# Feed-forward first products: one 512-column matmul for both parts of the activations

## The chip, the cores and the metric

The kernel runs on one core of a Trainium2 chip. The time is the device time of one execution, in microseconds (us); lower is better. The core has a matrix engine (TensorE, PE in the rows), whose weight loads have a row of their own (PEld), a vector engine (VectorE, DVE), a scalar engine (ScalarE, ACT), a third elementwise engine (GpSimd, POOL) and a queue that issues transfers (SyncE, SP). Each engine works off its own instructions in program order and waits on semaphores for the others.

## The reference

Activations are 256 tokens of 1024 channels. There are three layers with mixers of different kinds (a gated delta rule with pooling, a spatial gating unit, RWKV-7), and behind each mixer stands a feed-forward with a squared ReLU. The change concerns the three feed-forwards only:

```
D_MODEL = 1024
D_FF = 4 * D_MODEL
    ...
    u = rms_norm(h, norm_mlp[l])
    h = h + jnp.square(jax.nn.relu(u @ w_up[l])) @ w_down[l]
    ...
def _squared_relu_mlp(h, w1, w2):
    return jnp.square(jax.nn.relu(h @ w1)) @ w2
```

All inputs are float32.

## The kernel before

**Split products.** Matmul operands are rounded to a shorter format (float32r). To keep accuracy each operand is held as two such parts, a high part (the rounded value) and a low part (what the rounding left). A product is three matmuls: low weights by high activations, high weights by low activations, high by high. `split_matmul` (L2082 to L2086) issues them, all three into the same 256 columns of a PSUM bank; each loads its 128x128 weight tile anew.

**Units.** All weights come in units of 128 x 2048 numbers (1 MB) through a ring of four buffers. For each unit SyncE transfers it into `raw`, ScalarE rounds it to `w_high` (`high`, L660), VectorE forms `w_low` (`low`, L1237), TensorE uses it and counts `w_used`. `high(u)` waits until TensorE has used unit u-4, since the two share a buffer.

**A feed-forward.** The 4096 hidden channels go in 8 chunks of 512. A chunk has two up units (s = 0 and 1, two hidden tiles of 128 channels each, 8 input tiles deep, so 16 tile products of three matmuls, 48 in all) and two down units (`accumulate`, also 16 tile products). From unit u0 the ring holds: up chunk 0 (u0, u0+1), up chunk 1 (u0+2, u0+3), down chunk 0 (u0+4, u0+5), up chunk 2, down chunk 1, and so on. TensorE works in that order: `body(i)` does up chunk i+1, then down chunk i. The up results lie in banks 0 (s = 0) and 1 (s = 1), the down sums in banks 2 to 5; bank 6 takes the sum of squares for the token scale.

**Between the two products.** For each half s of a chunk ScalarE's `relu` (L862, L874 for chunk 0) takes the bank to `FB.r`, and with that the bank is free. VectorE's `hidden` squares it to `FB.h` (L1556), ScalarE's `square` makes the high part (L869), VectorE the low part (L1561). An up unit of chunk i+1 waits for `relu_done` of chunk i, half s.

**VectorE's order.** It is written out by hand. `mlp` does `low` of u0+2 and u0+3, halves the squares, does `low` of u0+4 and u0+5, and then for each chunk `body(i)`: `hidden(i)`, then `low` of the next four units: up chunk i+2 (two), down chunk i+1 (two). So `hidden(i)` stands behind the `low` of both down units of chunk i. In the second feed-forward `scale_lora` (L1618 to L1626) and the low part of a LoRA weight (L1581) stand between some chunks. ScalarE has the same order: `square` twice, `high` twice (up chunk i+2), `relu` twice (chunk i+1), `high` twice (down chunk i+1).

## Time and profile before

| | us |
|---|---|
| median of 3 runs | 1057.31 |
| lowest and highest | 1056.78, 1058.25 |
| span of the profiled execution (first to last instruction) | 1055.0 |
| TensorE matmul busy in it | 1038.3 |
| VectorE busy | 715.8 |
| ScalarE busy | 536.1 |

The profile is of one execution, whose span is 2.3 us under the median of the timed runs. Ends of matmuls are modelled and overlap, so TensorE's pace is read from the starts of its matmuls. Between first and last a timeline row gives start, length, engine, line and tiles; "x2" is two instructions of the same kind in a row, and the bracket behind a row is the idle time ahead of it and what ended it.

### The profile page before, as it was taken

The numbers are of one execution on the slowest core, as the hardware profiler recorded it, in microseconds if no ns is written. First come the engines' busy times: TensorE is split into PE (matmuls) and PEld (weight loads), VectorE is DVE, ScalarE is ACT, GpSimd is POOL, SyncE is SP. The second block draws the span as 40 slices with busy tenths as digits, with TensorE's granted clock in tenths as the row PEclk, the third lists the DMA queues.
The fourth block names the chain that finished last, engine by engine and source line by source line (L and its number), as shares of the span: only waits on it lengthen the run. The fifth ranks groups of instructions, "written<-read, shape, count | busy, mean of one in ns | idle before, by whom it ended". The sixth has DMA issues, their size and how long they took to land.

```text
span 1055.0 us, 21161 instructions
## 1 busy us (share of the span) xinstructions
PE 1038.3 (98%) x8984; PEld 1008.7 (96%) x8984; DVE 715.8 (68%) x1007; ACT 536.1 (51%) x639; POOL 32.6 (3%) x39
## 2 busy tenths in 40 slices
PE   7999999999999999999999999999999999999997
PEld 7999999999997899999999999999898999999997
DVE  6989665455567787666565567899978666555454
ACT  7847553434446464355445346897543255443431
POOL 0004000000000000000000000042000000000000
PEclk9999999999999999999999999999999999999999
DMA  9722475546744646565555553424100257555511
GB/s 293 222 81 82 160 262 177 194 166 203 275 157 141 219 160 204 159 186 211 186 172 184 182 191 120 140 73 152 58 2 2 64 179 253 183 189 171 196 40 40
DMA packets 119057, 167.01 MB, mean 158 GB/s; under 512 B 5840, under 2 KB 99664, under 8 KB 118608
## 3 DMA queue, kind: packets, MB, share of 16 engines
q1 hardware_dynamic: 117808, 165.92, 47.9%
q8 instruction: 48, 0.79, 0.3%
q10 hardware_dynamic: 1184, 0.17, 0.1%
q14 instruction: 17, 0.14, 0.0%
HBM read 165.03 MB, written 1.05 MB: 157 GB/s over the span
## 4 chain that ended last, share of the span: by engine, by line
PE 84%; DVE 10%; ACT 2%; issue 2%; SPq 1%; DMA 1%; DVEq 0%; ACTq 0%
PE banks L2084 25%; PE banks L2086 25%; PE banks L2085 24%; DVE sb_w_low L1237 2%; DVE sb_arena L1917 1%; DVE sb_state L1914 1%; DMA sb_raw<-in_w_in 1%; PE banks L2668 1%; PE banks L2535 1%; SPq L539 1%; PE banks L2779 0%; DVE sb_arena L1405 0%; DVE sb_state L1402 0%; PE banks L2838 0%; PE banks L2822 0%
## 5 line engine op out<-in xcount | busy, mean ns | idle before, releaser
L1237 DVE TENSOR_TENSOR sb_w_low<-sb_raw,sb_w_high 128x2048 fp32r<-128x2048 f32 x148 | 338.0, 2289 | 242.1 <-ACT sb_w_high L660 242.0
L660 ACT ACTIVATE sb_w_high<-sb_raw 128x2048 fp32r<-128x2048 f32 x148 | 281.8, 1911 | 262.9 <-PE banks L2086 261.7
L2084 PE MATMUL banks<-sb_act_high,sb_w_low 128*128 128x256 f32 x1352 | 386.3, 286 | 1.1 <-DVE sb_arena L1790 0.7
L2086 PE MATMUL banks<-sb_act_high,sb_w_high 128*128 128x256 f32 x1352 | 381.9, 282 | 0.0
L2085 PE MATMUL banks<-sb_act_low,sb_w_high 128*128 128x256 f32 x1352 | 380.0, 281 | 0.0
L2084 PEld LDWEIGHTS banks<-sb_act_high,sb_w_low 128*128 128x128 f32 x1352 | 254.6, 188 | 3.3 <-DVE sb_arena L1790 0.9
L2085 PEld LDWEIGHTS banks<-sb_act_low,sb_w_high 128*128 128x128 f32 x1352 | 255.9, 189 | 0.5 <-issue 0.2
L2084 PE MATMUL banks<-sb_hidden_high,sb_w_low 128*128 128x256 f32 x896 | 253.6, 283 | 0.0
L2086 PEld LDWEIGHTS banks<-sb_act_high,sb_w_high 128*128 128x128 f32 x1352 | 253.4, 187 | 0.0
L2086 PE MATMUL banks<-sb_hidden_high,sb_w_high 128*128 128x256 f32 x896 | 253.4, 283 | 0.0
L2085 PE MATMUL banks<-sb_hidden_low,sb_w_high 128*128 128x256 f32 x896 | 251.9, 281 | 0.0
L2085 PEld LDWEIGHTS banks<-sb_hidden_low,sb_w_high 128*128 128x128 f32 x896 | 169.5, 189 | 0.1
L2084 PEld LDWEIGHTS banks<-sb_hidden_high,sb_w_low 128*128 128x128 f32 x896 | 168.9, 189 | 0.1
L2086 PEld LDWEIGHTS banks<-sb_hidden_high,sb_w_high 128*128 128x128 f32 x896 | 167.8, 187 | 0.0
L1561 DVE TENSOR_TENSOR sb_hidden_low<-sb_arena,sb_hidden_high 128x512 fp32r<-128x512 f32 x48 | 31.2, 686 | 11.3 <-ACT sb_hidden_high L869 11.3
L869 ACT ACTIVATE sb_hidden_high<-sb_arena 128x512 fp32r<-128x512 f32 x48 | 27.6, 618 | 20.4 <-PE banks L2086 20.4
L1556 DVE TENSOR_TENSOR sb_arena<-sb_arena 128x512 f32<-128x512 f32 x48 | 30.7, 681 | 0.0
L2084 PE MATMUL banks<-sb_w_high,sb_act_low 128*128 128x512 f32 x64 | 26.3, 411 | 0.0
L2086 PE MATMUL banks<-sb_w_high,sb_act_high 128*128 128x512 f32 x64 | 25.4, 396 | 0.0
L2085 PE MATMUL banks<-sb_w_low,sb_act_high 128*128 128x512 f32 x64 | 25.3, 396 | 0.0
L633 POOL TENSOR_SCALAR sb_arena<-sb_arena 128x256 f32<-128x256 f32 x8 | 10.7, 1360 | 421.5 <-ACT sb_act_high L986 421.5
L862 ACT ACTIVATE sb_arena<-banks 128x512 f32<-128x512 f32 x42 | 22.3, 583 | 0.0
(443 smaller groups left out, 1048.6 us busy)
## 6 DMA issues: line engine op xcount, KB each, us to landing
sb_raw<-in_ffn_w SPq DMA_DIRECT2D x64, 1024.0 KB, 5.2
sb_raw<-in_w_up SPq DMA_DIRECT2D x16, 1024.0 KB, 5.4
sb_raw<-in_w_down SPq DMA_DIRECT2D x16, 1024.0 KB, 5.0
sb_raw<-in_sgu_w_in SPq DMA_DIRECT2D x16, 1024.0 KB, 5.3
sb_raw<-in_rwkv_w_rkv SPq DMA_DIRECT2D x12, 1024.0 KB, 5.2
sb_raw<-in_w_in SPq DMA_DIRECT2D x8, 1024.0 KB, 9.6
sb_raw<-in_sgu_w_out SPq DMA_DIRECT2D x8, 1024.0 KB, 4.9
sb_raw<-in_w_out SPq DMA_DIRECT2D x4, 1024.0 KB, 5.1
```

The costliest lines, as they stand in the source:

```text
L539: sp.dma_start(half_of(raw[j], t), w_in_v[:, :, c * 256 + t * P:c * 256 + t * P + P])\
L633: pool.tensor_scalar(RW.XS[:, k, :], RW.H[:, k, 1:T + 1], RW.omm[:, p:p + 1], None, ALU.mult)\
L660: nc.scalar.activation(whi[s][:], raw[s][:], ACT.Copy).then_inc(hi_done, 1)
L862: nc.scalar.activation(FB.r[:, 2 * s:2 * s + 2, :], two(bank[s][:]), ACT.Relu).then_inc(relu_done, 1)
L869: nc.scalar.activation(hid_hi[:, 2 * s:2 * s + 2, :], FB.r[:, 2 * s:2 * s + 2, :], ACT.Square)\
L1237: nc.vector.tensor_tensor(wlo[s][:], raw[s][:], f32(whi[s][:]), ALU.subtract).then_inc(lo_done, 1)
L1556: nc.vector.tensor_tensor(FB.h[:, hs, :], FB.r[:, hs, :], FB.r[:, hs, :], ALU.mult).then_inc(r_sq, 1)
L1561: nc.vector.tensor_tensor(hid_lo[:, hs, :], FB.h[:, hs, :], f32(hid_hi[:, hs, :]), ALU.subtract)\
L1914: base.add(nc.vector.tensor_tensor(tmp, RW.LB[:, j + 1:, j:j + 1].broadcast_to(shape), RW.WB[:, j:j + 1, 0:j + 1].broadcast_to(shape), ALU ...
L2084: nc.tensor.matmul(dst, l_lo, r_hi, start=start, stop=False, **kw)
L2085: nc.tensor.matmul(dst, l_hi, r_lo, start=False, stop=False, **kw)
L2086: return nc.tensor.matmul(dst, l_hi, r_hi, start=False, stop=stop, **kw)
```

## The change

The high and the low part of the activations become one tensor (`act_parts`). In an up unit each high weight tile is loaded once and meets both parts in one matmul of 512 columns, whose result fills a whole bank: high by high in the left 256 columns, high by low in the right. The low weights by high activations, 256 columns, are added to the right half. A half s of a chunk has two hidden tiles and thus takes two banks: 0 and 1 for s = 0, 6 and 7 for s = 1. The sum of squares moves to bank 5, which is also a down bank; so the first down unit waits at its seventh output tile until VectorE has taken the scale (`scale_taken`), and VectorE takes it in its first body, not in its last but one.

Behind the product ScalarE copies the right halves of both banks to `FB.r` (512 columns, as `relu` had), VectorE adds the left halves to it from PSUM (new, 48 instructions) and counts `up_taken`, then does ReLU and square in one instruction, ScalarE copies that to the high part, VectorE forms the low part. TensorE's up unit of chunk i+1 now waits for `up_taken` of chunk i, half s.

```diff
@@ scalar
-            def relu(i, s):
+            def copy_half(i, s):
                 act.wait_ge(w_used, i * 4 + (u0 - 2 + s + 1))
                 act.wait_ge(h_lo, i * 2 + (h0 - 2 + s + 1))
-                nc.scalar.activation(FB.r[:, 2 * s:2 * s + 2, :], two(bank[s][:]), ACT.Relu).then_inc(relu_done, 1)
-
-            def square(i, s):
-
-                act.wait_ge(relu_done, i * 2 + (16 * j + s + 1))
+                nc.scalar.activation(FB.r[:, 2 * s:2 * s + 2, :], up_halves[s][:, :, 1, :], ACT.Copy).then_inc(up_copied, 1)
+
+            def hidden_high(i, s):
+
+                act.wait_ge(r_sq, i * 2 + (16 * j + s + 1))
                 if not (type(i) is int and i == 0):
                     act.wait_ge(w_used, i * 4 + (u0 + s + 1))
-                nc.scalar.activation(hid_hi[:, 2 * s:2 * s + 2, :], FB.r[:, 2 * s:2 * s + 2, :], ACT.Square)\
+                nc.scalar.activation(hid_hi[:, 2 * s:2 * s + 2, :], FB.h[:, 2 * s:2 * s + 2, :], ACT.Copy)\
                     .then_inc(h_hi, 1)
@@ vector
             def hidden(i, then=lambda s: None):
                 for s in range(2):
                     hs = slice(2 * s, 2 * s + 2)
-                    dve.wait_ge(relu_done, i * 2 + (16 * j + s + 1))
-                    nc.vector.tensor_tensor(FB.h[:, hs, :], FB.r[:, hs, :], FB.r[:, hs, :], ALU.mult).then_inc(r_sq, 1)
+                    dve.wait_ge(up_copied, i * 2 + (16 * j + s + 1))
+                    nc.vector.tensor_tensor(FB.r[:, hs, :], FB.r[:, hs, :], up_halves[s][:, :, 0, :], ALU.add)\
+                        .then_inc(up_taken, 1)
+                for s in range(2):
+                    hs = slice(2 * s, 2 * s + 2)
+                    dve.wait_ge(up_taken, i * 2 + (16 * j + s + 1))
+                    nc.vector.scalar_tensor_tensor(FB.h[:, hs, :], FB.r[:, hs, :], 0.0, FB.r[:, hs, :], ALU.max,
+                                                   ALU.mult).then_inc(r_sq, 1)
...
-            def body(i, last):
+            def body(i, last, first=False):
                 hidden(i)
                 low(u0 + 6, i)
+                if first:
+                    token_scale()
                 low(u0 + 7, i)
@@ tensor
+                if n == 6 and scales is not None:
+                    pe.wait_ge(scale_taken, scales)
...
                 if i is not None:
-                    pe.wait_ge(relu_done, i * 2 + (16 * j + s + 1))
+                    pe.wait_ge(up_taken, i * 2 + (16 * j + s + 1))
                 for t in range(2):
                     for k in range(KT):
                         if first and t == 0 and s == 0:
                             pe.wait_ge(a_lo, a0 + k + 1)
-                        cs = slice(t * P, t * P + P)
-                        ins = split_matmul(bank[s][:, t * T:t * T + T], h[:, k, cs], l[:, k, cs], act_hi[:, k, :],
-                                           act_lo[:, k, :], start=k == 0, stop=k == KT - 1)
+                        cs, dst = slice(t * P, t * P + P), bank[UP_BANKS[s] + t]
+                        nc.tensor.matmul(two(dst[:]), h[:, k, cs], act_parts[:, :, k, :], start=k == 0,
+                                         stop=False, skip_group_check=True)
+                        ins = nc.tensor.matmul(dst[:, T:2 * T], l[:, k, cs], act_hi[:, k, :], start=False,
+                                               stop=k == KT - 1, skip_group_check=True)
```

TensorE, head of its loop over the chunks of the first feed-forward, from the last matmuls of down chunk 0 into up chunk 2; `relu` is the semaphore of `relu_done`. Before:

```order
L2085 MATMUL banks<-sb_hidden_low,sb_w_high 128x256
L2086 MATMUL banks<-sb_hidden_high,sb_w_high 128x256
L2474 UNCONDITIONAL_BRANCH
L2474 ISA
L2451 ISA [waits unit_low]
L2084 MATMUL banks<-sb_act_high,sb_w_low 128x256 [waits relu]
L2085 MATMUL banks<-sb_act_low,sb_w_high 128x256
L2086 MATMUL banks<-sb_act_high,sb_w_high 128x256
```

The same place in the changed kernel:

```order
L2102 MATMUL banks<-sb_hidden_low,sb_w_high 128x256
L2103 MATMUL banks<-sb_hidden_high,sb_w_high 128x256
L2495 UNCONDITIONAL_BRANCH
L2495 ISA
L2470 ISA [waits unit_low]
L2476 MATMUL banks<-sb_act_parts,sb_w_high 128x512 [waits up_taken]
L2478 MATMUL banks<-sb_act_parts,sb_w_low 128x256
```

Three matmuls of a tile product have become two, and the wait on ScalarE's `relu` has become one on VectorE's `up_taken`.

VectorE, first feed-forward, from `low` of the two units of down chunk 0 to the first chunk's `hidden` and the `low` behind it (`unit_high` is ScalarE's `high`, `hidden_hi` its high part of the hidden values). Before:

```order
L1237 TENSOR_TENSOR sb_w_low<-sb_raw,sb_w_high 128x2048 [waits unit_high] x2
L1584 UNCONDITIONAL_BRANCH
L1584 ISA
L1556 TENSOR_TENSOR sb_arena<-sb_arena 128x512 [waits relu]
L1555 REGISTER_ALU
L1556 TENSOR_TENSOR sb_arena<-sb_arena 128x512 [waits relu]
L1561 TENSOR_TENSOR sb_hidden_low<-sb_arena,sb_hidden_high 128x512 [waits relu_squared,hidden_hi] x2
L1236 ISA
L1237 TENSOR_TENSOR sb_w_low<-sb_raw,sb_w_high 128x2048 [waits unit_high]
```

The same place in the changed kernel:

```order
L1241 TENSOR_TENSOR sb_w_low<-sb_raw,sb_w_high 128x2048 [waits unit_high] x2
L1560 TENSOR_TENSOR sb_arena<-sb_arena,banks 128x512 [waits up_copied] x2
L1565 SCALAR_TENSOR_TENSOR sb_arena<-sb_arena 128x512 [waits up_taken] x2
L1571 TENSOR_TENSOR sb_hidden_low<-sb_arena,sb_hidden_high 128x512 [waits relu_squared,hidden_hi] x2
L1241 TENSOR_TENSOR sb_w_low<-sb_raw,sb_w_high 128x2048 [waits unit_high]
L1578 TENSOR_SCALAR sb_arena<-banks 128x256 [waits square_sums]
L1581 RECIPROCAL sb_arena<-sb_arena 128x256 [waits token_scale_taken]
L1241 TENSOR_TENSOR sb_w_low<-sb_raw,sb_w_high 128x2048 [waits unit_high] x3
```

The two adds that free the banks have come in at the place of the squares, behind the `low` of both down units; the token scale stands in the first body.

## Rows read from the trace of the kernel before

**Rows 1.** The page: busy time of the engines, share of the span, instructions.
```profile
PE 1038.3 (98%) x8984; PEld 1008.7 (96%) x8984; DVE 715.8 (68%) x1007; ACT 536.1 (51%) x639; POOL 32.6 (3%) x39
```

**Rows 2.** The page: the chain that ended last, by engine.
```profile
PE 84%; DVE 10%; ACT 2%; issue 2%; SPq 1%; DMA 1%; DVEq 0%; ACTq 0%
```

**Rows 3.** Groups by line: out<-in, count | busy us, mean ns | idle before, releaser.
```profile
L1237 DVE TENSOR_TENSOR sb_w_low<-sb_raw,sb_w_high 128x2048 fp32r<-128x2048 f32 x148 | 338.0, 2289 | 242.1 <-ACT sb_w_high L660 242.0
...
L1556 DVE TENSOR_TENSOR sb_arena<-sb_arena 128x512 f32<-128x512 f32 x48 | 30.7, 681 | 0.0
...
L1598 DVE TENSOR_TENSOR sb_arena<-banks,sb_arena 128x512 f32<-128x512 f32 x11 | 7.6, 689 | 10.8 <-PE banks L2086 10.8
...
L1689 DVE SCALAR_TENSOR_TENSOR sb_arena<-banks,sb_gating_scales,sb_arena 128x512 f32<-128x512 f32 x8 | 5.6, 744 | 0.0
```

**Rows 4.** Timeline, TensorE: first and 48th matmul of one up unit.
```profile
208.25 0.28 PE L2084 MATMUL banks<-sb_act_high,sb_w_low 128*128 128x256 f32 x1
...
213.89 0.28 PE L2086 MATMUL banks<-sb_act_high,sb_w_high 128*128 128x256 f32 x1
```

**Rows 5.** Timeline, TensorE: first and 93rd of the spatial gate's 512-column matmuls.
```profile
337.96 0.39 PE L2085 MATMUL banks<-sb_w_low,sb_act_high 128*128 128x512 f32 x1
...
359.50 0.40 PE L2084 MATMUL banks<-sb_w_high,sb_act_low 128*128 128x512 f32 x1
```

**Rows 6.** Timeline, TensorE: 256 columns behind 8-column weight loads, first and 22nd.
```profile
23.02 0.28 PE L2086 MATMUL banks<-sb_act_high,sb_ab_high 128*8 128x256 f32 x1
...
25.41 0.28 PE L2086 MATMUL banks<-sb_act_high,sb_ab_high 128*8 128x256 f32 x1
```

**Rows 7.** Timeline, ScalarE and VectorE around one chunk's `hidden`, loop of feed-forward 1.
```profile
198.75 1.06 ACT L862 ACTIVATE sb_arena<-banks 128x512 f32<-128x512 f32 x2
...
208.45 1.92 ACT L660 ACTIVATE sb_w_high<-sb_raw 128x2048 fp32r<-128x2048 f32 x1 [3.85 <-PE banks L2086]
...
210.40 2.29 DVE L1237 TENSOR_TENSOR sb_w_low<-sb_raw,sb_w_high 128x2048 fp32r<-128x2048 f32 x1 [3.47 <-ACT sb_w_high L660]
212.61 1.29 DVE L1556 TENSOR_TENSOR sb_arena<-sb_arena 128x512 f32<-128x512 f32 x2
```

**Rows 8.** Timeline, entry of feed-forward 1: TensorE's unit u0+2 begins; ScalarE; VectorE.
```profile
138.70 0.28 PE L2084 MATMUL banks<-sb_act_high,sb_w_low 128*128 128x256 f32 x1
...
139.39 3.71 ACT L660 ACTIVATE sb_w_high<-sb_raw 128x2048 fp32r<-128x2048 f32 x2
...
141.33 4.50 DVE L1237 TENSOR_TENSOR sb_w_low<-sb_raw,sb_w_high 128x2048 fp32r<-128x2048 f32 x2 [2.36 <-ACT sb_w_high L660]
145.75 1.29 DVE L1556 TENSOR_TENSOR sb_arena<-sb_arena 128x512 f32<-128x512 f32 x2
```

**Rows 9.** Timeline, VectorE in feed-forward 2: work between `low` and `hidden`.
```profile
521.53 2.29 DVE L1237 TENSOR_TENSOR sb_w_low<-sb_raw,sb_w_high 128x2048 fp32r<-128x2048 f32 x1 [3.47 <-ACT sb_w_high L660]
...
526.45 1.29 DVE L1556 TENSOR_TENSOR sb_arena<-sb_arena 128x512 f32<-128x512 f32 x2
...
546.78 2.42 DVE L1626 TENSOR_TENSOR sb_arena<-sb_arena,sb_vectors 128x512 f32<-128x512 f32 x3
...
569.82 2.28 DVE L1581 TENSOR_TENSOR sb_lora_low<-sb_arena,sb_lora_high 128x2048 fp32r<-128x2048 f32 x1
```

**Rows 10.** Timeline: a VectorE result and the TensorE matmul that waited for it.
```profile
860.53 0.48 DVE L1502 SCALAR_TENSOR_TENSOR sb_act_low<-sb_x,sb_vectors,sb_act_high 128x256 fp32r<-128x256 f32 x1
...
861.06 0.39 PE L2084 MATMUL banks<-sb_act_high,sb_w_low 128*128 128x256 f32 x1 [0.37 <-DVE sb_act_low L1502]
```

**Rows 11.** Windows (from:to length, PE busy (count), granted clock, DMA share, GB/s): the end.
```profile
1048.40:1051.30 2.90, 0.03 (x1) 1.00 0.14 47
1051.30:1055.00 3.70, 0.00 (x0) 0.50 0.75 247
```

**Rows 12.** Timeline, TensorE: first matmuls of the program; the last ones.
```profile
5.36 5.23 PE L2193 MATMUL banks<-sb_x,sb_ones 128*128 128x256 f32 x12 [5.36 <-DMA sb_x<-in_x_t]
...
1046.75 1.67 PE L2967 MATMUL banks<-sb_arena,sb_ones 128*128 128x256 f32 x7
```

More of the change, by code:

```diff
@@ L145, in place @@
         return nc.alloc_sbuf_tensor_at("sb_" + name, shape, dtype, offset=at + 4 * offset)
-    act_hi = place("act_high", 0, [P, KT, T], F32R)
-    act_lo = place("act_low", UNIT, [P, KT, T], F32R)
+    act_parts = place("act_parts", 0, [P, 2, KT, T], F32R)
+    act_hi, act_lo = act_parts[:, 0], act_parts[:, 1]
     hid_hi = place("hidden_high", 2 * UNIT, [P, 4, T], F32R)
@@ L355, in build_on @@
     FFN_ACC = [0, 6, 9]
+    UP_BANKS = [0, 6]
+    up_halves = [banks[:, 512 * b:512 * b + 1024].rearrange("p (t h n) -> p t h n", t=2, h=2) for b in UP_BANKS]
     ACC_SGU = 3
@@ L873, in mlp @@
                 act.wait_ge(w_used, u0 + s + 1)
-                nc.scalar.activation(FB.r[:, 2 * s:2 * s + 2, :], two(bank[s][:]), ACT.Relu).then_inc(relu_done, 1)
+                nc.scalar.activation(FB.r[:, 2 * s:2 * s + 2, :], up_halves[s][:, :, 1, :], ACT.Copy).then_inc(up_copied, 1)
             high(u0 + 4)
@@ L879, in body @@
                 for s in range(2):
-                    square(i, s)
+                    hidden_high(i, s)
                 high(u0 + 6, i)
@@ L889, in body_end @@
             def body_end(s):
-                square(FCH - 1, s)
+                hidden_high(FCH - 1, s)
                 if u0 + 4 * FCH < n_units:
@@ L1563, in hidden, with token_scale @@
                     then(s)
-            def body(i, last):
+            def token_scale():
+                dve.wait_ge(ss_done, SS[("ffn1", "ffn2", "ffn3")[j]] + 1)
+                nc.vector.tensor_scalar(FB.r2[j], bank[5][:, 0:T], 1.0 / D, EPS, ALU.mult, ALU.add)\
+                    .then_inc(scale_taken, 1)
+                dve.wait_ge(scale_taken, j + 1)
+                chain.add(nc.vector.reciprocal(FB.r2[j], FB.r2[j]))
+            def body(i, last, first=False):
                 hidden(i)
                 low(u0 + 6, i)
+                if first:
+                    token_scale()
                 low(u0 + 7, i)
@@ L1574, in mlp @@
                 for i in range(FCH - 2):
-                    body(i, False)
+                    body(i, False, first=i == 0)
                     if i in (1, 2):
@@ L1583, in mlp @@
             else:
-                with dve.Fori(0, FCH - 2) as i:
+                body(0, False, first=True)
+                with dve.Fori(1, FCH - 2) as i:
                     body(i, False)
-            dve.wait_ge(ss_done, SS[("ffn1", "ffn2", "ffn3")[j]] + 1)
-            chain.add(nc.vector.tensor_scalar(FB.r2[j], bank[6][:, 0:T], 1.0 / D, EPS, ALU.mult, ALU.add))
-            chain.settle()
-            chain.add(nc.vector.reciprocal(FB.r2[j], FB.r2[j]))
             body(FCH - 2, True)
@@ L2424, in _, with accumulate @@
             mixed_out(c, range(4, KT))
-        def accumulate(u, s, i=None, first=False, last=False):
+        def accumulate(u, s, i=None, first=False, last=False, scales=None):
             q = u % RING
@@ L2465, in body @@
                     pe.wait_ge(sq_folded, j + 1)
-                    nc.tensor.matmul(bank[6][:, 0:T], ones, FB.ss[j], start=True, stop=True).then_inc(ss_done, 1)
+                    nc.tensor.matmul(bank[5][:, 0:T], ones, FB.ss[j], start=True, stop=True).then_inc(ss_done, 1)
                 for s in range(2):
                     pe.wait_ge(h_lo, i * 2 + (h0 + s + 1))
-                    accumulate(u0 + 4 + s, s, i, first=first and s == 0)
+                    accumulate(u0 + 4 + s, s, i, first=first and s == 0, scales=j + 1 if first and s == 0 else None)
             up(u0, 0, first=True)
```

5 lines of the change are left out of this document (3 added, 2 removed).

## The prediction

> **What bounds the kernel now.** I read the page first. TensorE is busy 98% of the span, VectorE 68%, ScalarE 51% [rows 1], and the chain of work that ended last runs through TensorE for 84% [rows 2]. So the kernel goes at TensorE's pace, and a change is worth what it does to the starts of matmuls. Next, the timeline of one up unit: 48 matmuls of 256 columns, the first at 208.25, the last at 213.89, so 5.64/47 = 0.1200 us from start to start [rows 4]. No pause lies between the last down unit and this one. ScalarE and VectorE, on the other hand, wait: VectorE's `low` waited 242 us in all for ScalarE's `high` [rows 3], and the `high` at 208.45 had waited 3.85 us for TensorE to give its buffer back [rows 7]. This is slack, but it has a consequence for the order of things: the `high` and `low` of a down unit are tied to the moment at which TensorE finishes the down unit four earlier.
>
> **The merged matmuls.** A tile product was three matmuls, 3 x 0.1200 = 0.360 us. It becomes one of 512 columns and one of 256. The spatial gate has 512-column matmuls in the same format: 92 steps from 337.96 to 359.50, 0.2341 us each [rows 5]. So a tile product takes 0.2341 + 0.1200 = 0.3541 us, 5.9 ns less. There are 3 feed-forwards x 16 up units x 16 = 768, which gives 4.5 us. What goes is the part of a weight load that isn't hidden: behind loads of 8 columns the same 256-column matmul takes 2.39/21 = 0.1138 us [rows 6], 6.2 ns less than behind 128. The bounds: nothing, if the two separate runs of 256 columns in `act_parts` cost the 512-column matmul what it saves (a contiguous operand is all that rows 5 show); and 2 x 6.2 ns x 768 = 9.5 us, if the other load also vanishes behind the longer matmul. I take 4.5, since rows 5 measure it directly. The first 8 tile products of each feed-forward wait for activations anyway, so about 0.1 us of it is lost: 4.4.
>
> The Trainium skill (TensorE: Matmul & The Clock Gate, Back-to-back issue gap) gives for isolated matmuls a time of columns over 2.4 GHz plus 2.5 ns. By that a merged pair saves 2.5 ns, or 1.9 us in all, and my final sum would be 2.6 us higher; rows 4 and 5 (120.0 and 234.1 ns against its 109.2 and 215.8) lie above it, and I go by the rows.
>
> **The work that is added.** VectorE gets 48 adds out of PSUM, about 0.69 us each (same shape, L1598), and its 48 squares become instructions with three operands, 0.74 against 0.68 us [rows 3]: 33 + 3 = 36 us on an engine with 339 us idle. By volume this is hidden, since TensorE needs 23.0 us for a chunk (192 x 0.12) and VectorE some 12 (four `low` of 2.29 and four short ones). ScalarE's copies have the shapes of the ReLU and the square before and take their places.
>
> **The wait that is exchanged.** Here the time is decided. Up unit (i+1, s) may start only when the results of chunk i, half s, have left their banks. Before, ScalarE's ReLU did that, right behind the up unit and long before. Now VectorE's add does it, and that stands in `hidden(i)`, behind `low` of the two down units of chunk i. The second of these needs `high` of the same unit, and this needs TensorE to have finished the second down unit of chunk i-1. But this is the unit directly ahead of up unit (i+1, 0). So TensorE finishes a down unit, and the next thing it wants has yet to go through ScalarE (`high`), VectorE (`low`) and VectorE (add), one behind the other. What stands queued behind the waiting matmul is the whole rest of TensorE's program.
>
> The length is read off where these instructions already stand. In the loop, TensorE wants to start the up unit at 208.25 [rows 4]. ScalarE's `high` ran from 208.45, `low` from 210.40, and the squares, in whose place the adds come, from 212.61 [rows 7]. With 0.69 for an add the first bank pair is free at 213.30. From the end of a VectorE result to the matmul that waited for it lie 0.05 us (860.53 + 0.48 = 861.01, matmul at 861.06) [rows 10]. So TensorE restarts at 213.35: a **stall of 5.1 us**. The second half is free 0.6 us after the first, under cover of the 5.7 us of the first up unit. It happens for i = 1 to 6 in each of three feed-forwards: 18 x 5.1 = 91.8 us.
>
> At the entry (i = 0) TensorE wants unit u0+2 at 138.70. VectorE has `low` of u0+4 and u0+5 ahead, which end at 145.83, since ScalarE made their high parts in 139.39 to 143.10; the add would run from 145.75 to 146.44, the restart at 146.49 [rows 8]. That is 7.8 us; the entries of the other two feed-forwards show the same offsets. 3 x 7.8 = 23.4 us.
>
> In feed-forward 2 more work stands between `low` and `hidden`: from 521.53 to 526.45 are 4.92 us, where the loop has 2.21 (210.40 to 212.61), so 2.7 more; the second group of three (2.42, net 2.3) and two LoRA low parts (2.28, net 2.2 each) follow in the next three chunks [rows 7, 9]. Together 9.4 us. The stalls sum to 91.8 + 23.4 + 9.4 = **124.6 us**.
>
> That the engine can't slip the adds in earlier is what the rows show: the squares at 212.61 had had their input since ScalarE's two ReLUs ended at 199.8 and still ran behind the `low` [rows 7]. The Trainium skill (TensorE: Matmul & The Clock Gate, Architectural detail) has the same as a rule against the change: VectorE and ScalarE take their queues strictly in order. By that the stalls are certain; with a free order the sum would be that of the first rival.
>
> **The clock.** After the last matmul, whose modelled end is 1048.4, the granted clock stood at 1.00 until 1051.3 and then fell to 0.50 [rows 11], 1.2 GHz in place of 2.4, 2.9 us after work had stopped. The stalls are 5.1 us and more, so it will mostly fall in them. What comes back how fast, only the start shows: the first twelve matmul instructions started 0.44 us apart ((5.23 - 0.4)/11), from 5.36 to about 10.2, the last ones of the same form 0.22 apart ((1.67 - 0.38)/6, with 0.38 for the length of one) [rows 12]: 4.9 us at half pace, 2.4 us lost. Per stall the loss is between 0 (clock stays, or falls just as work resumes and returns at once) and 2.4. I take 1.7, nearer the upper end, since the stall is nearly twice the 2.9 us but a restart need not meet the full 4.9. 21 x 1.7 = **35.7 us**; bounds 0 and 50.4.
>
> The Trainium skill (same page, Part 1: The HAM clock gate) says that throttled is the default and activity releases it; with that rule alone the loss would be above zero at each of the 21 restarts.
>
> **Edits at nothing.** The first down unit waits at its seventh tile for `scale_taken`. That is 36 x 0.12 = 4.3 us after its start, while the sum of squares is ready at its start, and VectorE by then waits for the next `high`; covered, and if not, under 2 us each, three times. The longer way to the low part of the hidden values (copy, add, square, copy, low part, some 3.4 us) lies beside the up units of chunk i+1, 11.3 us, which start only after the first add. No transfer moves on SyncE's queue; each is due a chunk ahead.
>
> **Sum**, against the profiled execution: 1055.0 - 4.4 + 124.6 + 35.7 = 1210.9 us of span; with the 2.3 us by which the median lies above it, **1213 us**.
>
> **Rivals.**
> *No stall (faster).* If the adds were reached in time, only the merged matmuls would show: 1057.3 - 4.4 = 1052.9, or between 1047.8 and 1057.3 with the bounds. It decides at one point: VectorE's `low` of a chunk's second down unit would have to end 5.1 us before it does, ahead of the end of the down unit before it. For it: before the change TensorE never waited here, and VectorE is idle a third of the time. Against: rows 7, where idle time is all ahead of `low` and not ahead of the squares. 6%.
> *Stalls, but the clock stays.* 1057.3 - 4.4 + 124.6 = 1177.5. For it: the one fall that the trace has came at a real end, and when in a pause it comes may vary; the start's slow pace might have to do with something else. Against: 2.9 us is well under 5.1, and the row at 0.50 is plain. 12%. A clock that falls in half of the stalls gives about 1195 and belongs to the forecast's range.
> *Stalls, and the full price of the clock at each.* 1213.3 + 14.7 = 1228; if besides each stall is 0.3 us longer (ScalarE or VectorE slower to start than in rows 7), 1234. 12%.
>
> **How the numbers follow.** The forecast, stalls with a clock that mostly falls, has 68% and by itself lies between 1192 and 1228. Another 2% is left for something not seen. For 8 in 10 the range must take in one side case whole: it goes down to 1175 (clock stays) and up to 1236. The measurement can tell about 0.2% (2 us) from no change; only the first rival is not slower, and it is faster by over 0.2% in most of its bounds. Faster 0.05, same 0.02, slower 0.93.
>
> **What would show it.** In the profile of the changed kernel: TensorE waits for VectorE's add (L1560) 21 times, some 125 us in all, none over 9 us; a chunk takes 28 to 30 us where it took 23; within an up unit a tile product takes 0.354 us; granted clock at 0.50 for a stretch behind most stalls. It would be wrong if TensorE's idle time before the merged matmuls is small, if the clock column stays at 1.00, or if up units are slower than 0.36 us per tile product at full clock.

## The result

The changed kernel takes 1228.9 us (median of 4 runs, 1227.1 to 1230.8) against 1057.2 us (4 runs, 1056.8 to 1058.3): a ratio of 1.1621, 95% interval 1.1607 to 1.1635. It is 16% slower. The forecast was 1213 us, the range 1175 to 1236.

The profiled execution has a span of 1227.2 us. Its page: busy time, the granted clock in 40 slices, the chain that ended last by engine, and the costliest group (count | busy us, mean ns | idle before, releaser).

```profile
PE 1088.2 (89%) x8216; PEld 1009.6 (82%) x8216; DVE 747.3 (61%) x1055; ACT 540.0 (44%) x639; POOL 32.6 (3%) x39
...
PEclk9999888888899999988888889999999988888889
...
PE 76%; DVE 13%; ACT 5%; issue 4%; SPq 1%; DMA 1%; DVEq 0%; ACTq 0%
...
L2476 PE MATMUL banks<-sb_act_parts,sb_w_high 128*128 128x512 f32 x768 | 323.0, 453 | 122.1 <-DVE sb_arena L1560 121.7
```

Beside [rows 1, 2]: TensorE's share fell from 98 to 89%, though it has 768 matmuls fewer and more busy time (a slow clock makes each of them longer). In the chain, VectorE and ScalarE together went from 12 to 18%. The clock's row has 8s in three stretches, which are the three feed-forwards. Nearly all idle time of the new matmul has one releaser, the add, and the view of TensorE's waits (total us, times, longest) counts it:

```profile
PE banks L2476 <- DVE sb_arena L1560: 121.7, 21, 7.7
```

The timeline around one of the 21 waits, in the loop of feed-forward 1 (start, length, engine, line, ..., idle time before): TensorE's last matmul of a down unit and its next one; ScalarE; VectorE.

```profile
202.25 0.28 PE L2103 MATMUL banks<-sb_hidden_high,sb_w_high 128*128 128x256 f32 x1
207.45 0.80 PE L2476 MATMUL banks<-sb_act_parts,sb_w_high 128*128 128x512 f32 x1 [4.92 <-DVE sb_arena L1560]
...
202.57 1.91 ACT L664 ACTIVATE sb_w_high<-sb_raw 128x2048 fp32r<-128x2048 f32 x1 [3.84 <-PE banks L2103]
...
204.51 2.29 DVE L1241 TENSOR_TENSOR sb_w_low<-sb_raw,sb_w_high 128x2048 fp32r<-128x2048 f32 x1 [3.46 <-ACT sb_w_high L664]
206.72 1.28 DVE L1560 TENSOR_TENSOR sb_arena<-sb_arena,banks 128x512 f32<-128x512 f32 x2
```

These lines answer to [rows 7]. The chain is to be read from top to bottom: TensorE ends a down unit, this lets ScalarE's `high` start (202.57), then `low` (204.51), then the adds (206.72), and after the first of them TensorE goes on at 207.45. From its last start, 202.25, that is 5.20 us, of which 0.12 would have passed anyway. In the same way the 21 places sum to 127.5 - 21 x 0.12 = 125.0 us of stopped TensorE.

The windows of the same stop (from:to length, PE busy (count), granted clock, DMA share, GB/s):

```profile
202.30:206.30 4.00, 0.23 (x2) 1.00 0.71 256
206.30:207.40 1.10, 0.00 (x0) 0.54 0.00 0
207.40:213.20 5.80, 5.75 (x18) 0.50 0.54 181
213.20:221.40 8.20, 8.20 (x49) 1.00 0.00 0
```

The last matmul's modelled end is 202.53; 3.9 us later the clock fell from 2.4 to 1.2 GHz, and it stayed there for the first 5.8 us of the up unit. Over the 21 stops the fall came 2.4 to 4.6 us behind the last start. Added up from windows of 0.2 us, TensorE worked 114.9 us at the half clock behind the 21 restarts: 3.8 to 6.2 us behind each, 5.5 in the mean.

What the half clock does to a tile product is seen in the same up unit: first two starts at half clock, six tile products apart, then an up unit's first matmul and the one behind its last, 16 tile products apart, at full clock.

```profile
208.26 0.63 PE L2476 MATMUL banks<-sb_act_parts,sb_w_high 128*128 128x512 f32 x1
...
212.10 0.63 PE L2476 MATMUL banks<-sb_act_parts,sb_w_high 128*128 128x512 f32 x1
...
215.76 0.39 PE L2476 MATMUL banks<-sb_act_parts,sb_w_high 128*128 128x512 f32 x1
...
221.36 0.28 PE L2101 MATMUL banks<-sb_hidden_high,sb_w_low 128*128 128x256 f32 x1
```

3.84/6 = 0.640 us against 5.60/16 = 0.350 us. So of 114.9 us at the half clock a share of 1 - 0.350/0.640 = 0.453 is lost, 52.1 us.

### The profile page after: what moved, and what is told of

Same layout as the page of the kernel before. It is cut to its first block, busy times and chain, and to the rows that moved or that the text cites. A ratio compares the mean times of both kernels' runs of the same rounds, so it can differ in the third digit from the quotient of the medians.

```text
span 1227.2 us, 19655 instructions
## 1 busy us (share of the span) xinstructions
PE 1088.2 (89%) x8216; PEld 1009.6 (82%) x8216; DVE 747.3 (61%) x1055; ACT 540.0 (44%) x639; POOL 32.6 (3%) x39
## 4 chain that ended last, share of the span: by engine, by line
PE 76%; DVE 13%; ACT 5%; issue 4%; SPq 1%; DMA 1%; DVEq 0%; ACTq 0%
PE banks L2476 18%; PE banks L2101 14%; PE banks L2103 13%; PE banks L2102 13%; PE banks L2478 9%; DVE sb_w_low L1241 4%; ACT sb_w_high L664 4%; DVE sb_arena L1560 1%; DVE sb_arena L1934 1%; DVE sb_state L1931 1%; DMA sb_raw<-in_w_in 1%; PE banks L2689 1%; PE banks L2556 1%; SPq L543 1%; DVE sb_arena L1643 0%
## 5 line engine op out<-in xcount | busy, mean ns | idle before, releaser
L2476 PE MATMUL banks<-sb_act_parts,sb_w_high 128*128 128x512 f32 x768 | 323.0, 453 | 122.1 <-DVE sb_arena L1560 121.7
L2476 PEld LDWEIGHTS banks<-sb_act_parts,sb_w_high 128*128 128x128 f32 x768 | 169.8, 221 | 170.1 <-DVE sb_arena L1560 102.2
L2478 PE MATMUL banks<-sb_act_parts,sb_w_low 128*128 128x256 f32 x768 | 237.1, 309 | 0.0
L2101 PE MATMUL banks<-sb_act_parts,sb_w_low 128*128 128x256 f32 x584 | 169.4, 290 | 0.8 <-DVE sb_arena L1807 0.7
L2478 PEld LDWEIGHTS banks<-sb_act_parts,sb_w_low 128*128 128x128 f32 x768 | 170.0, 221 | 0.0
L2103 PE MATMUL banks<-sb_act_parts,sb_w_high 128*128 128x256 f32 x584 | 164.9, 282 | 0.0
L2102 PE MATMUL banks<-sb_act_parts,sb_w_high 128*128 128x256 f32 x584 | 164.0, 281 | 0.0
L2101 PEld LDWEIGHTS banks<-sb_act_parts,sb_w_low 128*128 128x128 f32 x584 | 109.8, 188 | 2.8 <-DVE sb_arena L1807 0.9
L2102 PEld LDWEIGHTS banks<-sb_act_parts,sb_w_high 128*128 128x128 f32 x584 | 110.8, 190 | 0.5 <-issue 0.2
L2103 PEld LDWEIGHTS banks<-sb_act_parts,sb_w_high 128*128 128x128 f32 x584 | 109.4, 187 | 0.0
L1565 DVE SCALAR_TENSOR_TENSOR sb_arena<-sb_arena 128x512 f32<-128x512 f32 x48 | 30.9, 684 | 0.0
L1560 DVE TENSOR_TENSOR sb_arena<-sb_arena,banks 128x512 f32<-128x512 f32 x48 | 30.7, 680 | 0.0
```

The source lines that it names most:

```text
L1560: nc.vector.tensor_tensor(FB.r[:, hs, :], FB.r[:, hs, :], up_halves[s][:, :, 0, :], ALU.add)\
L1565: nc.vector.scalar_tensor_tensor(FB.h[:, hs, :], FB.r[:, hs, :], 0.0, FB.r[:, hs, :], ALU.max, ALU.mult).then_inc(r_sq, 1)
L2101: nc.tensor.matmul(dst, l_lo, r_hi, start=start, stop=False, **kw)
L2102: nc.tensor.matmul(dst, l_hi, r_lo, start=False, stop=False, **kw)
L2103: return nc.tensor.matmul(dst, l_hi, r_hi, start=False, stop=stop, **kw)
L2476: nc.tensor.matmul(two(dst[:]), h[:, k, cs], act_parts[:, :, k, :], start=k == 0, stop=False, skip_group_check=True)
```

## The experiments

All times are medians, beside runs of the kernel before on the same chip (1057.0 to 1057.9 us). "With early adds" is the first kernel below.

### The adds moved ahead

In the changed kernel, VectorE's adds leave `hidden` and stand ahead of the `low` of u0+8. That is the first down unit of chunk i+1 (the expectation has the number right and calls it the second of chunk i), so both `low` that stood ahead of the adds now stand behind them. At a feed-forward's entry, not in the cut below, one add goes ahead of the halving of the squares and one behind it, both ahead of the `low` of u0+4.

```diff
             def hidden(i, then=lambda s: None):
-                for s in range(2):
-                    ... add of the two halves, .then_inc(up_taken, 1)
             def body(i, last, first=False):
                 ...
                 low(u0 + 7, i)
+                for s in range(2):
+                    take(i + 1, s)        # the same add
                 if not last:
                     low(u0 + 8, i)
```

> The changed kernel with one thing moved: VectorE's two adds of chunk i+1's halves stand ahead of the low work of the second down unit of chunk i (unit u0+8) instead of behind it; in chunk 0 one stands ahead of the halving and one behind it. Nothing else differs. Theory (TensorE waits only for VectorE's place in line, and the slow clock is a result of these waits): the 21 waits for the add go (at most some 0.5 us is left at an entry), the granted clock is 1.00 to the last matmul, and what is left is the merging alone, 768 tile products at 0.350 us in the place of 0.360: 1057.2 - 7.7 = 1049.5 us (1048.5 to 1051). Rival A (the merged matmul itself, its eight accumulators' banks or the second PSUM operand on VectorE cost something that the waits cover): over 1057 us, with the loss spread over the up units. Rival B (the move only shifts the wait to the halving or to ScalarE's high, which is now later): some of the 125 us comes back as waits for the weights' low part, 1055 to 1100 us.

Measured: 1050.0 us (1049.9 to 1052.0), ratio 0.9934, interval 0.9921 to 0.9948, span 1048.3. It is 0.7% faster than the kernel before. Its page, and the adds in the timeline:

```profile
PE 1030.5 (98%) x8216; PEld 965.3 (92%) x8216; DVE 746.9 (71%) x1055; ACT 538.0 (51%) x639; POOL 32.6 (3%) x39
...
PEclk9999999999999999999999999999999999999999
```

```profile
197.78 2.29 DVE L1241 TENSOR_TENSOR sb_w_low<-sb_raw,sb_w_high 128x2048 fp32r<-128x2048 f32 x1 [2.84 <-ACT sb_w_high L664]
199.99 1.28 DVE L1553 TENSOR_TENSOR sb_arena<-sb_arena,banks 128x512 f32<-128x512 f32 x2
203.54 2.29 DVE L1241 TENSOR_TENSOR sb_w_low<-sb_raw,sb_w_high 128x2048 fp32r<-128x2048 f32 x1 [2.27 <-ACT sb_w_high L664]
```

The adds now fill 1.2 of the 3.5 us in which VectorE waited for `high` ahead of the `low` of u0+8 (the idle time there is 2.27 us in place of 3.47). VectorE and ScalarE do as much as in the changed kernel, and TensorE waits for them nowhere in a loop. So the whole of the loss, 1227.2 - 1048.3 = 178.9 us of span, comes from the place of two instructions: 125.0 us of stops, and 53.9 us that is left. The slow work counted above makes 52.1 of it, and the next but one experiment asks whether it is the clock. Rivals A and B fall.

### The place of the wait in the kernel before

The kernel before, with nothing of the change but a wait of the same kind:

```diff
                 if i is not None:
-                    pe.wait_ge(relu_done, i * 2 + (16 * j + s + 1))
+                    pe.wait_ge(r_sq, i * 2 + (16 * j + s + 1))
```

> The kernel before, with one wait exchanged: an up unit of TensorE waits for VectorE's square of chunk i, which stands where the changed kernel has its adds, instead of ScalarE's relu. No merged matmul, no other bank, no second PSUM operand. Theory (the loss is the place of VectorE's instruction in its queue and nothing of the merging): 21 waits of nearly the length seen in the changed kernel and its clock loss, 1057.2 + 125 + 55 = 1237 us, or 1225 to 1245 as the wait may end up to 0.6 us earlier or later than there. Rival (the merged form causes a good part of the loss): well under 1200 us.

Measured: 1234.4 us (1233.8 to 1235.7), ratio 1.1678 (1.1660 to 1.1696), span 1231.9. TensorE's waits:

```profile
PE banks L2084 <- DVE sb_arena L1556: 127.9, 21, 7.7
```

No merged matmul, no other bank, no add, and the same loss. From start to start, less 0.12 us each, the 21 stops sum to 131.3 us; the three at the last chunks of the feed-forwards are 7.3 us in place of 5.2. For the clock 1231.9 - 1055.0 - 131.3 = 45.6 us are left, beside 99.3 us of work at the half clock; at 0.360 us for a tile product in place of 0.640 that loses 43.4. The rival falls.

### The stops filled with work

In the changed kernel, TensorE gets matmuls of zeros once a chunk, ahead of the wait of its first up unit:

```diff
             def body(i, first=False):
+                for _ in range(60 if first else 40):
+                    nc.tensor.matmul(bank[2][:, 0:T], zeros_r[:], act_hi[:, 0, :], start=first, stop=False, ...)
                 for s in range(2):
                     up(u0 + 2 + s, s, i)
```

> The changed kernel; ahead of each up unit's wait for the add TensorE is given work that changes nothing: 40 matmuls (60 at a feed-forward's first chunk) of a tile of zeros onto an accumulator, 0.12 us each at full clock, 4.8 us and 7.2 us. The adds come when they came before, since nothing that VectorE or ScalarE waits for is moved. Theory (the clock falls because TensorE stands still, and that costs 2.6 us a wait): the starts of the up units are as late as before but the clock stays at 1.00, so 1228.9 - 55 = 1174 us, 1172 to 1178. Rival (the 55 us are something else in the merged units, such as their own pitch, or the filler comes on top of the wait): 1229 us or more.

Measured: 1180.3 us (1178.3 to 1181.5), ratio 1.1163 (1.1144 to 1.1181), span 1176.3. A window over more than a chunk, and the filler ahead of an up unit:

```profile
195.00:235.00 40.00, 39.72 (x287) 1.00 0.45 157
```

```profile
169.22 4.96 PE L2486 MATMUL banks<-sb_act_parts,sb_zeros 128*128 128x256 f32 x40
174.37 0.50 PE L2478 MATMUL banks<-sb_act_parts,sb_w_high 128*128 128x512 f32 x1 [0.20 <-DVE sb_arena L1562]
```

The up unit still starts when the add is done: from the last matmul of a down unit to the first of the up unit the 21 places sum to 125.2 us (0.12 taken off each, the filler counted in). But the clock stays at 1.00 in 20 of the 21, and 49 us are gone. So the clock is the cause of the second term.

The one place where it falls is among four in feed-forward 2 whose stops are so long (7.5 to 8.0 us) that 40 fillers leave a wait:

```profile
664.30:666.50 2.20, 0.00 (x0) 1.00 0.57 151
666.60:670.00 3.40, 3.31 (x10) 0.50 0.50 204
```

From start to start 2.7 us of standing still (664.01 to 666.69) were enough there, while gaps of 2.7, 2.8 and 3.2 us at the other three left the clock alone.

The span lies 1176.3 - 1048.3 = 128.0 us above that with early adds, 3.0 more than the stops of the changed kernel: 0.2 are in the stops, some 1.5 in the 3.3 us of slow work at that place, and the rest wasn't placed. The run is 6.3 us above the 1174 I had expected, and 2.3 above the upper end of 1178: 3.0 are those of the span, 2.3 come from the median's distance to it (4.0 here, 1.7 in the changed kernel), and 1.1 because I had put 55 us for the clock where 53.9 were left.

### What the clock's part depends on

Four kernels change the length of the stops. Two have one more instruction on VectorE ahead of each chunk's adds in the changed kernel: of 1.2 us,

```diff
             def hidden(i, then=lambda s: None):
+                nc.vector.tensor_scalar(x[:], x[:], 1.0, None, ALU.mult)
```

> The changed kernel with one more instruction on VectorE ahead of each chunk's adds: the activations (128 x 2048) times 1.0 in place, about 2.1 us. Theory (each wait is VectorE's queue, one for one, and the clock price per wait no longer grows with the wait's length): 21 x 2.1 = 44 us more, 1273 us, the clock loss still about 55 us in all. Rival (the clock price grows with the length of the wait): up to 21 x 2 us above that, 1315 us. Rival (VectorE has slack, the queue is not what TensorE waits for): under 1240 us.

or of 2.25 us.

```diff
             def hidden(i, then=lambda s: None):
+                nc.vector.scalar_tensor_tensor(x[:], x[:], 1.0, x[:], ALU.mult, ALU.max)
```

> The changed kernel with one instruction on VectorE of about 2.25 us (the larger of the activations and the activations, 128 x 2048, in place) ahead of each chunk's adds, where the one of 1.14 us had made every wait 1.13 us longer and yet lowered the clock loss from 2.6 to 2.0 us a wait. The waits become 2.25 us longer: 21 x 2.25 = 47 us. Theory (the loss depends on where the stop falls against the moments at which the clock can change, not on its length): 1228.9 + 47 = 1276 us give or take 21 x 1.5 us, the loss at 1.5 to 3.5 us a wait and the same in nearly all of them. Rival A (the loss shrinks with the length): at 1.4 us a wait, 1251 us. Rival B (a constant 2.6 us): 1276 us sharp.

The other two put the adds of the kernel with early adds a little later in its loop, which brings 18 of the 21 waits back at a shorter length.

```diff
                 if not last:
                     low(u0 + 8, i)
+                    dve.wait_ge(hi_done, (i * 4 + (u0 + 10)))
+                for s in range(2):
+                    take(i + 1, s)
+                if not last:
                     low(u0 + 9, i)
```

> The kernel with the early adds, but in the loop the adds of chunk i+1 stand behind the low work of unit u0+8 and behind a wait for ScalarE's high of unit u0+9, so that 18 of the 21 waits are back, at about 2.9 us each in place of 5.2; the entries have none. Theory (the clock falls some 3 to 5 us after the last matmul, so a wait of 2.9 us is at the border): without a fall 1049.5 + 18 x 2.9 = 1102 us; with the full price of 2.6 us for each, 1149 us. I expect the clock to stay at 1.00 in most of them, 1102 to 1115 us. Rival (every stop of TensorE of any length costs the clock): 1149 us.

```diff
                 low(u0 + 7, i)
+                if not last:
+                    dve.wait_ge(hi_done, (i * 4 + (u0 + 9)))
+                ... twice: x = max(x * 1.0, x), 128x2048
                 for s in range(2):
                     take(i + 1, s)
```

> The kernel with the early adds, but in the loop VectorE waits for ScalarE's high of unit u0+8 and then takes twice the larger of the activations and the activations (128 x 2048, in place, 2.27 us each) ahead of chunk i+1's adds. With 1.14 us there the adds began at 206.21 in the trace, the first ended at 206.85, and the second down unit's last matmul starts at about 208.5, so there was no wait at all; with 4.5 us the first add ends 3.4 us later, at 210.2: 18 waits of about 1.6 us. Theory (the clock falls only behind a longer stop than this): 1050.0 + 18 x 1.6 = 1079 us, granted clock 1.00. Rival (each stop costs what one of 3.0 us did, 1.6 us): 1079 + 29 = 1108 us.

Measured. The stops are summed from start to start less 0.12 us each; "left" is the span less 1048.3 us (early adds) and less the stops. "Slow work" is TensorE's busy time where the granted clock is 0.50 behind the stops, and in brackets what is lost by it, 0.453 of it.

| kernel | us | span | stops in the loop | sum of stops | left | left per stop | slow work |
|---|---|---|---|---|---|---|---|
| adds after two multiplications | 1085.2 (1085.0 to 1086.6) | 1084.6 | 1.7 us | 18: 30.3 | 6.0 | 0.3 | 0 |
| adds behind `low` of u0+8 | 1133.8 (1132.6 to 1134.3) | 1130.7 | 3.0 | 18: 53.4 | 29.0 | 1.6 | 57.4 (26.0) |
| changed kernel | 1228.9 (1227.1 to 1230.8) | 1227.2 | 5.1 | 21: 125.0 | 53.9 | 2.6 | 114.9 (52.1) |
| 1.2 us more | 1242.8 (1241.4 to 1244.2) | 1239.3 | 6.2 | 21: 148.8 | 42.2 | 2.0 | 86.6 (39.3) |
| 2.25 us more | 1267.8 (1267.0 to 1269.5) | 1264.9 | 7.3 | 21: 171.2 | 45.4 | 2.2 | 95.9 (43.4) |

Where the clock falls, the slow work accounts for what is left but for 2 to 3 us. The stops grow as VectorE's work does, 23.8 us for 21 x 1.13 and 46.2 for 21 x 2.2, so each wait is VectorE's queue, one for one. My 1273 us for the first was 30 us too high: 20 by the length of its instruction (I had put 2.1 us, the trace has 1.22, a net 1.13), and some 12 because the clock's part fell from 53.9 to 42.2 where I had it unchanged. But the clock's part doesn't grow with the stop. It is nothing at 1.7 us, 1.6 at 3.0, largest at 5.1, and smaller again beyond. At 3.0 us I had expected it to stay away in most places, 1102 to 1115 us, and was wrong; the rival's full price at each, 1149 us, was too much. At 1.7 us the clock held, as expected, and the rival of 1108 us falls. Windows from these kernels, in the order of the table:

```profile
212.30:213.80 1.50, 0.01 (x1) 1.00 0.00 0
213.80:222.00 8.20, 8.20 (x47) 1.00 0.49 183
```

```profile
244.80:247.80 3.00, 0.17 (x3) 1.00 0.82 330
...
247.80:248.40 0.60, 0.60 (x3) 0.99 0.11 41
248.40:251.70 3.30, 3.30 (x12) 0.50 0.00 0
...
943.00:954.00 11.00, 8.22 (x57) 1.00 0.56 181
```

```profile
204.30:206.90 2.60, 0.00 (x0) 1.00 0.82 331
206.90:210.30 3.40, 0.00 (x0) 0.50 0.38 64
210.30:213.60 3.30, 3.26 (x10) 0.50 0.73 298
213.60:220.00 6.40, 6.40 (x38) 0.99 0.00 0
```

```profile
213.30:219.00 5.70, 5.66 (x17) 0.50 0.29 121
242.80:246.00 3.20, 0.00 (x0) 0.51 0.50 111
246.00:249.60 3.60, 3.59 (x11) 0.50 0.47 192
```

Behind the stop of 1.7 us the clock is at 1.00. With 3.0 us, in the place shown, it stays at 1.00 through the stop (244.8 to 247.8) and falls 0.6 us after TensorE has gone back to work. It is so in 11 of the 18 places, where it falls 0.06 to 0.8 us behind the restart; in six it falls in the last 0.3 us of the stop, and in one, the stop from 946.27 to 949.33, not at all (943 to 954). With 1.2 us more it falls 2.9 us into the stop, so that about half of the slow stretch passes while nothing runs, and 3.3 us of work are slow in place of 5.8. With 2.25 us more, two neighbouring stops of the same length (7.41 and 7.40 us from start to start) are followed by 5.7 and by 3.6 us of slow work. So what a stop costs in clock isn't a function of its length alone: it varies with the moment of the fall and of the return, by a factor of 1.6 between these two. Rival A for that kernel (1251 us, shrinking with the length) and rival B (a constant 2.6) both fall; that the loss would be the same in nearly all stops, as my theory said, is wrong as well. Which moment a given stop meets, I can't tell ahead from its length.

Of the 6.0 us left with stops of 1.7 us, about 2 are the chunks themselves (24.49 us from start to start, against the 22.72 with early adds + 1.66), 1.8 are three waits for the hidden values' low part, and the rest wasn't placed.

A fifth kernel of this kind made no stop:

```diff
                 low(u0 + 7, i)
+                if not last:
+                    dve.wait_ge(hi_done, (i * 4 + (u0 + 9)))
+                nc.vector.tensor_scalar(x[:], x[:], 1.0, None, ALU.mult)
                 for s in range(2):
                     take(i + 1, s)
```

> The kernel with the early adds, but in the loop VectorE waits for ScalarE's high of unit u0+8 and multiplies the activations (128 x 2048) by 1.0 in place (1.14 us) ahead of chunk i+1's adds: 18 waits of TensorE of about 1.9 us each, none at the entries. The wait of 3.0 us cost 1.6 us of clock loss beside its own length. Theory (the clock falls only behind a longer stop): 1050.0 + 18 x 1.9 = 1084 us and a granted clock of 1.00. Rival (every stop costs about as much): 1084 + 18 x 1.6 = 1113 us.

Measured: 1051.7 us (1051.5 to 1051.9), ratio 0.9942 (0.9928 to 0.9957), and no wait in the loop. I had counted from the wrong `high`: that of u0+8 needs only the first down unit's end, and the second down unit, 5.8 us of TensorE's work, still lies ahead of the up unit. VectorE in the timeline:

```profile
205.06 1.23 DVE L1595 TENSOR_SCALAR sb_x<-sb_x 128x2048 f32<-128x2048 f32 x1 [3.46 <-ACT sb_w_high L664]
206.21 1.28 DVE L1553 TENSOR_TENSOR sb_arena<-sb_arena,banks 128x512 f32<-128x512 f32 x2
```

The adds start at 206.21, 3.1 us behind the start of `high` at 203.11, where with early adds they start 1.6 us ahead of it (199.99 and 201.59). That is 4.7 us later, and it costs 1.7 us in all at most (0.8 by the two ratios). So the early place has room to spare.

### What the merging gains

In the kernel with early adds, the 512-column matmul is split again, with everything else of the change kept:

```diff
-                        nc.tensor.matmul(two(dst[:]), h[:, k, cs], act_parts[:, :, k, :], ...)
+                        nc.tensor.matmul(dst[:, 0:T], h[:, k, cs], act_hi[:, k, :], ...)
+                        nc.tensor.matmul(dst[:, T:2 * T], h[:, k, cs], act_lo[:, k, :], ...)
                         ins = nc.tensor.matmul(dst[:, T:2 * T], l[:, k, cs], act_hi[:, k, :], ...)
```

> The kernel with the early adds, but each 512-column matmul is split again into two of 256 columns with the same weight tile (accumulators, banks, adds and order as in the kernel with the early adds; 2304 matmuls in the up units in place of 1536). Theory (the whole gain of the merging is the tile product's 0.350 against 0.360 us, the new bank layout and the work on VectorE and ScalarE cost nothing on the path): 1057.2 us again, 7.7 us above the kernel with early adds, pitch 0.120 us in the up units. Rival (part of the shorter tile product comes from the layout, the writes of two accumulators, and not from the number of matmuls): nearer to 1050 us.

Measured: 1058.3 us (1057.3 to 1058.7, 11 runs), ratio 1.0006 (0.9997 to 1.0015): the same as before. The next has the second of the three load 8 columns of weights only:

```diff
-                        nc.tensor.matmul(dst[:, T:2 * T], h[:, k, cs], act_lo[:, k, :], ...)
+                        nc.tensor.matmul(dst[0:8, T:2 * T], h[:, k, t * P:t * P + 8], act_lo[:, k, :], ...)
```

> The kernel with three matmuls of 256 columns for a tile product (two halves), but the second of them loads only 8 columns of the high weight tile and so computes only 8 of its 128 output rows; the output is not the reference's. Number and columns of the matmuls are those of the kernel with two halves, the weight loads those of the merged form plus 8 columns. Theory (the merged form gains by the load that it spares: two full loads beside 768 columns): about 1050 us, as with the early adds. Rival A (it gains by the matmul that it spares, whatever is loaded): 1058 us, as with two halves. Rival B (both, by the pitch of 0.1138 us that matmuls of 8 loaded columns have among each other in the kernel before): 768 x 6.2 ns less than 1058.3, 1053.5 us.

Measured: 1058.5 us (12 runs, 1056.4 to 1065.0), ratio 1.0013 (0.9998 to 1.0027). Two starts 29 tile products apart with early adds, then two that are 19 apart with the small load (TensorE's timeline, an up unit's first matmul lines; between them only up units):

```profile
207.85 0.39 PE L2482 MATMUL banks<-sb_act_parts,sb_w_high 128*128 128x512 f32 x1
...
218.00 0.39 PE L2482 MATMUL banks<-sb_act_parts,sb_w_high 128*128 128x512 f32 x1
```

```profile
209.24 0.28 PE L2482 MATMUL banks<-sb_act_parts,sb_w_high 128*128 128x256 f32 x1
...
216.08 0.28 PE L2482 MATMUL banks<-sb_act_parts,sb_w_high 128*128 128x256 f32 x1
```

10.15/29 = 0.350 us and 6.84/19 = 0.360 us. The small load gains nothing (rival A's time): the saving isn't in the size of the load. It comes when a matmul and its weight load go as instructions; which of the two it is, no run separates. Between two halves and merged lie 8.3 us, 10.8 ns for each of the 768, of which the starts show 10. Two more kernels ask whether order or layout has a part in it: the two matmuls exchanged, and the 512 columns from one contiguous run (edits in short).

```diff
-  two(dst[:]) with h and act_parts, then dst[:, T:2 * T] with l and act_hi
+  dst[:, T:2 * T] with l and act_hi, then two(dst[:]) with h and act_parts
```

> The kernel with the early adds, the two matmuls of a tile product in the other order: 256 columns with the low weights first, then 512 columns with the high weights. It tells what the tile product's 0.350 us hangs on, where I had reckoned 0.120 + 0.234 = 0.354. Theory (a pitch is set by a matmul's own columns, whichever tile was ahead): again 0.350 us and 1049.5 us. Rival (in the given order the load of the low tile hides behind 512 columns, and the load of the next high tile behind 256; this is the same in a circle either way, so another number would speak for a cost at the change of accumulator): off by over 2 us from the kernel with early adds.

```diff
-  nc.tensor.matmul(two(dst[:]), h[:, k, cs], act_parts[:, :, k, :], ...)
+  nc.tensor.matmul(two(dst[:]), h[:, k, cs], act_parts[:, 0, 2 * (k // 2):2 * (k // 2) + 2, :], ...)
```

> The kernel with the early adds, but the 512 columns of the merged matmul are read from one contiguous run of the high activations (two neighbouring k tiles) and not from two runs of 256 that lie 8 KB apart; only the first 8 of a feed-forward's tile products keep the two runs. The accumulators then hold products with the wrong parts of the activations, so the output is not the reference's, while number, size and order of all instructions are kept. Theory (a moving operand in two runs is read as fast as one run): 1049.5 us as with the early adds. Rival (the jump between the runs costs some ns a matmul, which would explain any part of the 512 columns' price over twice 256): 1 to 4 us less.

Measured: 1050.5 us (1049.8 to 1051.2), ratio 0.9932 (0.9917 to 0.9947), and 1051.1 us (1049.7 to 1051.4), ratio 0.9934 (0.9917 to 0.9950). Neither matters.

## Why the prediction held, and where it was off

**The stops: right, in mechanism and size.** I had reckoned 124.6 us from where `high`, `low` and the squares stood in the trace of before; it came to 125.0. In the loop 5.1 us were expected, and the starts are 5.19 to 5.27 us apart with 0.12 to be taken off; at the entries 7.8, measured 7.9 (7.98 less 0.12). In feed-forward 2 the two groups of three and the two LoRA low parts were to add 9.4 us, and the gaps of 7.97, 7.60, 7.46 and 7.46 in place of 5.26 add 2.7 + 2.3 + 2.2 + 2.2 = 9.4. The trace has 21 waits, none over 9 us, all for the add, as the list of signs had it. The Trainium skill (TensorE: Matmul & The Clock Gate, Architectural detail) says that VectorE takes its queue strictly in order; the runs agree, since the same add costs nothing when the program puts it ahead of `low` and 179 us of span when it stands behind.

**The clock: the mechanism right, the term mis-sized.** The step was "I take 1.7, nearer the upper end, since the stall is nearly twice the 2.9 us but a restart need not meet the full 4.9". The 21 restarts met 3.8 to 6.2 us at the half clock, 5.5 in the mean, and lost 2.6 us each, 53.9 us in place of 35.7 (52.1 of it counted as slow work). Even the upper bound of 2.4 was a little too low. It came from the length of the slow stretch at the program's start, one sample; the experiments show that this length varies with the moment (3.8 to 6.2 us of slow work in the changed kernel alone). That the clock falls in the stops was right in all 21 places. The rival with the full price, 1228 us, had the better number, in part by luck, since two of its errors partly cancel: 50.4 us for the clock and 4.4 for the merging, against 53.9 and 6.7.

**The merged matmuls: the term mis-sized.** The step was 0.2341 + 0.1200 = 0.3541 us for a tile product, each price taken from a stream of its own kind; it is 0.350. Over the up units that is 7.7 us, where 4.5 was forecast; the spans give 1055.0 - 1048.3 = 6.7, the medians 7.3. My reason for the gain, the part of a load of 128 columns that isn't hidden, falls with the kernel that loads 8 columns and gains nothing. [rows 6], where all matmuls in a row have small loads, remains unexplained by it. The lower bound's reason, two runs of columns costing more than one, isn't there either.

**Edits at nothing: right.** VectorE's 36 us (31.5 in the trace), ScalarE's copies, the new wait of the first down unit and the layout of banks cost nothing that can be measured: with them and without the merging the time is that of before (ratio 1.0006, 0.9997 to 1.0015).

**The sum.** 1055.0 - 6.7 + 125.0 + 53.9 = 1227.2 us of span, which closes by the way 53.9 was found (with the 52.1 counted it is 1.8 short); forecast were 1055.0 - 4.4 + 124.6 + 35.7 = 1210.9. Of the 16.3 us between them the clock makes 18.2, the stops 0.4, and the merging takes 2.3 back. A chunk takes 30.5 us (202.25 to 232.76 from last start to last start), a little over the 28 to 30 expected, by the same clock.

## What to carry to other kernels

When a wait is handed from one engine's instruction to another's, read where the new one stands in its own queue, and what that queue needs in turn; if it needs what the waiting engine has just finished, TensorE stands still for the whole chain at each turn, and its length can be read off to a few tenths of a microsecond before anything is run. The remedy is a place and not less work: two adds moved ahead of two `low` turn +16% into -0.7%. Where TensorE is the bound, the clock added about half of the stops' own sum at 3.0 and 5.1 us, over a quarter where they were longer, and nothing at 1.7. So price it with a range, and see whether work can stand in the stop.

## What the runs showed of the chip that I had not expected

- The clock can fall after TensorE is back at work: up to 0.8 us behind the end of a stop of 3.0 us, and then 3.4 us at the half clock. It fell in 17 of 18 stops of 3.0 us and in one of four that the filler left at 2.7 to 3.2 us; stops of 1.7 us left it alone in all 18 places.
- A longer stop can cost less clock: 2.6 us a stop at 5.1 us, 2.0 at 6.2.
- At the half clock a tile product of 768 columns takes 0.640 us, 1.83 times the 0.350 at the full one and not twice as much. The Trainium skill (TensorE: Matmul & The Clock Gate, "Wait — 56ns, not 53.3ns?") says that matmuls follow each other by exactly their columns over 1.2 GHz at the slow clock, and by columns over 2.4 GHz plus some 2.5 ns at the fast one. The first agrees: 768/1.2 GHz is 0.640 us. The second doesn't: by it the product would take 0.325 us, and the trace has 0.350 merged and 0.360 with three matmuls.
- A matmul's price depends a little on its neighbour: 0.350 us is 4 ns below the sum of the two prices measured apart. Over feed-forward 1 with early adds the mean from a 512-column matmul's start to the next is 233.2 ns and from a 256-column one's 117.6, against 234.1 and 120.0 apart; in the exchanged order it is 232.3 and 118.6. So the larger part is with the 256 columns. Why, and what the 10.8 ns of a spared matmul are made of, stays open; it is not the size of the weight load, not the order, not the operand's layout.
